# Reordering the routing stage of two MoE phases: early weight splits, weight loads, spare products, first gather

## What is computed

```
t = rmsnorm(h)
grp_prob = softmax(t @ w_grp + b_grp);  p_g, g_idx = top_k(grp_prob, 1)       # 4 groups
q_top, e_local = top_k(softmax(logits of 8 experts in the group), 2)
gates = p_g * q_top / sum(q_top)
for every expert e (32):  y = (silu(x @ w_gate[e]) * (x @ w_up[e])) @ w_down[e]   # 1024 -> 512 -> 1024
h = h + sum over the two chosen experts of gate * y
```

## Time and profile before

| | |
|---|---|
| median of three runs | 2169.26 us (2168.65 to 2170.42) |
| the profiled execution's own time | 2169.74 us |
| its span | 2167.6 us |
| TensorE busy | 1953.3 us, 90% |
| VectorE busy | 1580.9 us, 73% |
| ScalarE busy | 1252.3 us, 58% |
| GpSimd busy | 383.1 us, 18% |
| DMA | 504.67 MB, mean 233 GB/s |
| first instructions of phase 1 and phase 2 | 400.2 us, 1464.4 us |

### The profile page before, as it was taken

The page is one execution under the profiler, slowest core; times in us unless marked ns, Lnnn a source line. Parts: engine busy times, 40 slices in busy tenths (PEclk is TensorE's granted clock), DMA queues, the critical chain, the costliest instruction groups (busy, mean ns, idle before and its releaser), DMA issues. The chain is left out here.

```text
span 2167.6 us, 31724 instructions
## 1 busy us (share of the span) xinstructions
PE 1953.3 (90%) x10658; PEld 1564.4 (72%) x10658; DVE 1580.9 (73%) x1765; ACT 1252.3 (58%) x1530; POOL 383.1 (18%) x677
## 2 busy tenths in 40 slices
PE   4859999849999999999699999995799999999991
PEld 3648777637888888888588766664688888888880
DVE  8996321358999999999752476646588888888885
ACT  6624210427887788888530265534477777777772
POOL 2000000302322222221233000002122222222214
PEclk9979999869999999999799999997799999999995
DMA  3174200529999999999612110006499999999986
GB/s 102 28 70 158 89 1 1 196 95 350 373 386 379 380 381 378 386 389 388 232 53 56 45 45 2 1 1 255 157 357 360 370 380 380 384 383 388 383 310 243
DMA packets 136044, 504.67 MB, mean 233 GB/s; under 512 B 38466, under 2 KB 68498, under 8 KB 84754
## 3 DMA queue, kind: packets, MB, share of 16 engines
q1 hardware_dynamic: 114658, 468.71, 59.1%
q0 software_dynamic: 18432, 33.86, 4.1%
q10 hardware_dynamic: 2880, 1.12, 0.4%
HBM read 488.47 MB, written 47.32 MB: 247 GB/s over the span
## 5 line engine op out<-in xcount | busy, mean ns | idle before, releaser
L1704 DVE TENSOR_TENSOR moe_lo<-moe_raw,moe_hi 128x2048 fp32r<-128x2048 f32 x378 | 860.9, 2292 | 106.8 <-ACT moe_hi L1483 98.1
L1483 ACT CAST moe_hi<-moe_raw 128x2048 fp32r<-128x2048 f32 x374 | 713.4, 1916 | 144.5 <-PE moe_ps_g L1854 67.2
L1852 PE MATMUL moe_ps_g<-moe_hi,moe_x_hi 128*128 128x512 f32 x512 | 210.4, 411 | 7.7 <-DVE moe_x_lo L1709 4.7
L1852 PE MATMUL moe_ps_y<-moe_hi,moe_h_hi 128*128 128x512 f32 x512 | 207.1, 404 | 3.8 <-DVE moe_h_lo L1720 3.8
L1854 PE MATMUL moe_ps_g<-moe_lo,moe_x_hi 128*128 128x512 f32 x512 | 204.1, 399 | 0.0
L1853 PE MATMUL moe_ps_g<-moe_hi,moe_x_lo 128*128 128x512 f32 x512 | 203.9, 398 | 0.0
L1854 PE MATMUL moe_ps_y<-moe_lo,moe_h_hi 128*128 128x512 f32 x512 | 202.1, 395 | 0.0
L1853 PE MATMUL moe_ps_y<-moe_hi,moe_h_lo 128*128 128x512 f32 x512 | 201.8, 394 | 0.0
L1854 PE MATMUL moe_ps_u<-moe_lo,moe_x_hi 128*128 128x512 f32 x512 | 201.2, 393 | 0.0
L1852 PE MATMUL moe_ps_u<-moe_hi,moe_x_hi 128*128 128x512 f32 x512 | 200.8, 392 | 0.0
L1853 PE MATMUL moe_ps_u<-moe_hi,moe_x_lo 128*128 128x512 f32 x512 | 200.8, 392 | 0.0
(11 more groups left out here) (457 smaller groups left out, 3749.9 us busy)
## 6 DMA issues: line engine op xcount, KB each, us to landing
moe_raw<-moe_w_gate SPq DMA_DIRECT2D x128, 1024.0 KB, 7.0
moe_raw<-moe_w_up SPq DMA_DIRECT2D x128, 1024.0 KB, 8.0
moe_raw<-moe_w_down SPq DMA_DIRECT2D x128, 1024.0 KB, 7.5
mix_r<-ssm_w_glu SPq DMA_DIRECT2D x16, 512.0 KB, 5.3
xn_dram<-moe_work SPq DMA_DIRECT2D x16, 512.0 KB, 7.2
prj_yc<-y_dram SPq DMA_DIRECT2D x8, 1024.0 KB, 7.0
moe_raw<-y_dram SPq DMA_DIRECT2D x8, 1024.0 KB, 11.0
mix_r<-x SPq DMA_DIRECT2D x8, 512.0 KB, 5.4
```

The costliest lines, as they stand in the source:

```text
L1483: A.copy(hi[:, slot(number, k), :], raw[:, k, :]).then_inc(hi_done, 1)
L1704: V.tensor_tensor(lo[:, slot, :], raw[:, k, :], hi[:, slot, :].bitcast(F32), ALU.subtract).then_inc(lo_done, 1)
L1852: T.matmul(out, x_h, w_h, start=first, stop=False)
```

## The change

- VectorE waits for the router's bias in `logits(0)`, TensorE for the router's weights in `tile_logits(0)`, not ahead of the loop.
- ScalarE does the squares two tiles ahead.
- `EARLY` is (2, 4, 6), and the six weight loads stand behind the stores of tiles 0, 1, 3, 5, 6, 7 (`LOADS`).
- TensorE makes 8 products of the identity with itself (`spare_products`) ahead of the tile loop and 18 ahead of its register load. Their result is not used.
- The first gather takes its rows from `idx_in[:, 0:1]` directly, without `column`.
- The transposes, the cast and the subtraction of the first expert tile go in two halves; the first piece of the gate product waits for the first half alone.

```
@@ names
+        x0_mm, x0_hi, x0_lo = (sem(x) for x in ("x0_mm", "x0_hi", "x0_lo"))
...
-        EARLY = (5, 6, 7)
+        EARLY = (2, 4, 6)
+        LOADS = (0, 1, 3, 5, 6, 7)
@@ sync
                 sp.dma_start(xn_dram[i * P:i * P + rows(i), :], xn[0:rows(i), i % XB, :]).then_inc(xn_out[i % XB], 16)
-                if i < NB:
-                    load(i, 0)
+                if i in LOADS:
+                    load(LOADS.index(i), 0)
@@ gpsimd
-            def gather(tile, step):
-                column(gi, idx_in, tile, step)
+            def gather(index):
                 G_.indirect_dma_start(xg[:, :], None, xn_dram[:, :],
-                                      bass.IndirectOffsetOnAxis(gi[:, :].bitcast(U32), 0),
+                                      bass.IndirectOffsetOnAxis(index.bitcast(U32), 0),
...
-            gather(0, 1)
+            pool.wait_ge(rows_ready, 1)
+            gather(idx_in[:, 0:1])
             pool.wait_ge(list_ready, 2)
             n_q = pool.value_load(n_more[0:1, 0:1], min_val=0, max_val=XTR) + N_EXP
             for tile in range(1, 3):
                 pool.wait_ge(xt_mm, tile)
-                gather(tile, tile + 1)
+                column(gi, idx_in, tile, tile)
+                gather(gi[:, :])
...
@@ scalar
             squares(0)
+            squares(1)
             for i in range(NT):
-                if i + 1 < NT:
-                    squares(i + 1)
+                if i + 2 < NT:
+                    squares(i + 2)
...
-            x_hi_part(0)
+            act.wait_ge(x0_mm, 1)
+            A.copy(x_hi[:, 0:KC, :].rearrange("p c m -> p (c m)"), ps_xt[:, 0:512]).then_inc(x0_hi, 1)
+            act.wait_ge(xt_mm, 1)
+            A.copy(x_hi[:, KC:, :].rearrange("p c m -> p (c m)"), ps_xt[:, 512:]).then_inc(xt_hi, 1)
@@ vector
-            dve.wait_ge(b_rt_in, 32)
 
             def logits(i):
+                if i == 0:
+                    dve.wait_ge(b_rt_in, 32)
                 dve.wait_ge(lg_mm, i + 1)
...
-            x_lo_part(0)
+            for q, (ready, done) in enumerate(((x0_hi, x0_lo), (xt_hi, xt_lo))):
+                dve.wait_ge(ready, 1)
+                part = slice(KC * q, KC * (q + 1))
+                V.tensor_tensor(x_lo[:, part, :].rearrange("p c m -> p (c m)"), ps_xt[:, 512 * q:512 * (q + 1)],
+                                x_hi[:, part, :].bitcast(F32).rearrange("p c m -> p (c m)"),
+                                ALU.subtract).then_inc(done, 1)
@@ tensor
+            def spare_products(n):
+                for _ in range(n):
+                    T.matmul(ps_u[:, 0:P], ident[:], ident[:], start=True, stop=True)
+
             pe.wait_ge(ident_step, 2)
-            pe.wait_ge(rt_in, 32)
+            spare_products(8)
 
             def tile_logits(i):
+                if i == 0:
+                    pe.wait_ge(rt_in, 32)
...
             last.then_inc(slot_mm, 1)
+            spare_products(18)
             pe.wait_ge(list_ready, 2)
...
-            def transpose_x(e):
+            def transpose_x(e, halves=False):
...
+                    if halves and c == KC - 1:
+                        last.then_inc(x0_mm, 1)
...
-                pe.wait_ge(xt_lo, e + 1)
+                if not halves:
+                    pe.wait_ge(xt_lo, e + 1)
                 for k in range(4):
+                    if halves and k < 2:
+                        pe.wait_ge((x0_lo, xt_lo)[k], 1)
...
-            transpose_x(0)
-            gate_up(0, lambda k: 2 + k, [(2 + k) % 3 for k in range(4)])
+            transpose_x(0, halves=True)
+            gate_up(0, lambda k: 2 + k, [(2 + k) % 3 for k in range(4)], halves=True)
```

More of the change, by code:

```diff
@@ L1429, in _ @@
                 pool.wait_ge(xt_mm, tile)
-                gather(tile, tile + 1)
+                column(gi, idx_in, tile, tile)
+                gather(gi[:, :])
             with pool.Fori(1, n_q - 2) as e:
                 pool.wait_ge(xt_mm, e + 2)
-                gather(e + 2, e * 2 + 2)
+                column(gi, idx_in, e + 2, e * 2 + 1)
+                gather(gi[:, :])
                 pool.wait_ge(y_done, e)
-                scatter(e - 1, e * 2 + 3)
+                scatter(e - 1, e * 2 + 2)
             for last in range(3):
                 pool.wait_ge(y_done, n_q + (last - 2))
-                scatter(n_q + (last - 3), n_q * 2 + (last - 2))
+                scatter(n_q + (last - 3), n_q * 2 + (last - 3))
             if last_layer:
@@ L1854, in products, with gate_up @@
                 return T.matmul(out, x_h, w_l, start=False, stop=final)
-            def gate_up(e, number, slots):
-                pe.wait_ge(xt_lo, e + 1)
+            def gate_up(e, number, slots, halves=False):
+                if not halves:
+                    pe.wait_ge(xt_lo, e + 1)
                 for k in range(4):
+                    if halves and k < 2:
+                        pe.wait_ge((x0_lo, xt_lo)[k], 1)
                     pe.wait_ge(lo_done, number(k) + 1)
```

## The result

The changed kernel takes **2156.93 us** (median of 12 runs; eleven lie between 2153.92 and 2161.79, and one slow run of 2187.62 us is not compared), against 2168.86 us for the kernel before, run beside it on the same chip (12 runs, 2166.46 to 2173.89). The ratio is 0.9946, 95% interval 0.9939 to 0.9953: 11.9 us faster, where 12.2 were forecast. The profiled execution took 2154.48 us, its span is 2152.4 us.

A forecast was written before the change was run, and what follows sets the result against it. It took the expert loop as TensorE-bound and unchanged, with the gains ahead of it: 1.7 + 3.8 + 1.5 + 0.4 + 2.7 + 2.1 = 12.2 us, giving 2157.0 us; range 2152 to 2164.

The forecast's parts named there:

- Entry: Start of each phase's tile loop: transposes of tile 2 (T2) start 2.4 us sooner in phase 1, 3.2 in phase 2.
- Pauses: Tile loop: 1.5 us before transposes of tiles 4, 6, 8; 4.5 us in phase 1, 3.0 in phase 2.
- rival 3: Tile loop: the pauses drop the clock, five at 1.6 us are 8.0 us, 2165.0 us; chance 0.08.
- First load: Cast at tile 2: wait for its weight load between 0 and 3.5 us, taken as 0.
- Transposes of the first expert: Seam: transposes start after 18 spare products (6.0 us) and register load (0.8): 465.15 against 464.48, phase 2 1526.0 against 1524.27.
- Chain in halves: First expert's first transposes to first product: 2.15 us against 4.33; product 1.5 us sooner, phase 2 0.4.
- Clock: First 48 products of the first expert, all at full clock: 2.7 us saved in phase 1, 2.1 in phase 2.
- Rival 1: Seams: 18 spare products at low clock take 8.1 us, outlast the wait; seams lose 4.2 us, 2161.2 us; chance 0.12.
- Rival 2: Tile loop: GpSimd falls behind VectorE, rstd of tiles 5 and 7 late, 4 us, 2161.0 us; chance 0.08.
- Rival 4: Tile loop: clock stays low from tile 4's pause to the end; change slower, net +13, 2182 us; chance 0.03.

The follow-up runs named there:

- the second profile: The changed kernel itself, unedited, timed again beside the kernel before: 2154.85 us, ratio 0.9935.
- the last run: Changed kernel with router-bias wait back ahead of VectorE's loop, router-weights wait ahead of the first transposes, behind the 8 spare products: 2159.75 us, ratio 0.9959.

## Why the prediction was right, point by point

- **Entry.** Forecast 2.4 and 3.2 us for T2; measured 3.22 and 3.10. In phase 1 the 8 products were through at the start of T0 (404.00), and T0 itself ran partly at full clock (1.59 us). The 0.7 us charged for their own time was too much: it is 0 to 0.6 us. The run without them puts their return at 0.4 to 1.4 us per phase, that time included.
- **Pauses.** Forecast 1.5 us each, on the scaling behind a subtraction; measured 1.31, 1.24, 1.23 and 1.52, 1.24. In phase 1 the clock then fell for 1.5 us at L7, which the forecast had left to rival 3; in the second profile it did not. Entry and pauses together: forecast 1.7 and 3.8, measured 1.5 and 4.0.
- **First load.** Forecast no wait; it held in phase 1 with almost nothing to spare, as the last run showed, and within 0.2 us in phase 2. Here luck helped: the forecast's own range for this wait was 0 to 3.5 us. Its remark that SP passes 1 MB at tiles 2 and 4 is a slip, since only the 0.5 MB store is left there.
- **Transposes of the first expert.** Here a step failed: "The register load, 0.48 + 0.16 us on the weight-load queue plus gaps, 0.8 in all, was hidden under the gather and no longer is." It runs while the spare products do, and costs nothing: a term of 1.6 us over both seams that should have been zero. With 5.69 and 6.18 us for the products, where 6.0 was forecast, they start 0.74 us sooner in phase 1 and 0.78 later in phase 2, instead of 0.7 and 1.7 later. The start in phase 1 also needs the sooner gather, which the forecast had put at nothing, hidden under the products: they end at about the time it lands.
- **Chain in halves.** Forecast 2.15 us; measured 2.12 and 2.00. The first product came 3.0 and 1.5 us sooner, against 1.5 and 0.4 forecast: 2.6 us too little. The register load is 1.6 of it, the shorter row of phase 1 another 0.3, and the rest are hand-overs.
- **Clock.** Forecast 2.7 and 2.1 us; measured 2.72 and 1.87. With 6 slow products in both phases, the low end of the 6 to 14 that the Trainium skill gives for one kernel (TensorE: Matmul & The Clock Gate, "What's actually happening"), it would have been 2.2 together, by estimate; the trace measured 4.6. The page does not call 6 the usual count, as the prediction took it.
- **Not forecast.** The tile from the second to the third expert's transposes takes 1.1 us more in phase 1 and 0.25 in phase 2. Its window was 18.64 us at a granted clock of 0.91 before, and 19.77 at 0.83 after. TensorE waits the same in both, 2.96 us for VectorE's `moe_hid` and 1.52 us for a subtraction; only the granted clock behind the first of them differs, 0.88 before and 0.78 after. Both lengths came with a fast and with a slow start of the 48 products ahead of it: 18.64 us in the run with the waits behind the 8 products, whose 48 were fast, and 20.19 without the 18 products, whose 48 were slow. So it is not shown to be the change's doing. It took back 1.4 us, nearly what the register load had given.

So the sum of 12.2 came out at 13.2 by stages and 11.9 by medians. That it came so near is in part luck: the seams returned 2.6 us more than forecast and the second expert's tile took 1.4 back. Rival 1 is half true: in phase 2 the spare products do outlast the gather, by 1.1 to 1.6 us, but they took 5.69 and 6.18 us and not 8.1. Rival 2 did not come up in the changed kernel. Rival 3 came at one pause of five in one profile, 1.5 us and not 8.0. Rival 4 did not come up. What stays open is how much of the 11.9 the late gathers move: one stands in the profile of the kernel before, seven in that of the kernel without the 8 products, and none in either profile of the changed kernel.

Not all parts of the change pay. Against the medians of the changed kernel, squares two ahead are worth 4.5 to 6.6 us (a late load in phase 2 included), the moved waits 2.8 to 4.9, the 8 products 1.2 to 3.2 (1.3 to 1.8 by stages). The 18 products are worth 3.6 to 3.9 us by stages (1.7 by medians) and the halves 5.9 (1.5 to 3.6 by medians); these two overlap, since each needs the other. The direct first gather is worth an estimated 0.7. The placement of splits costs 3.1 us with the squares ahead and 6.0 without. With the scaling ahead of the subtraction that cost is gone, and the kernel takes 2148.83 us. This order with 12 spare products in phase 2 was not run; by an estimate from the stages it should give another 0.8.

## What to carry to other kernels

A step that is spread out to relieve an engine costs its full pause at each place, if it stands in the queue ahead of work for which the next engine waits; put that work first, and then spreading pays. Filling a wait with spare products is free only as far as the wait reaches, so measure the wait in every phase, and look in the trace whether the clock stays up over the wait behind them. Before charging an instruction on a side queue to the path, look whether the main unit has work queued ahead of it.

## What the runs showed of the hardware

- A register load on TensorE's weight-load queue (0.49 us) ran under products that had been issued before it; the transposes followed the last product with no gap.
- Pauses of TensorE of 1.2 to 1.5 us left the clock up in most cases, with a dip behind the third of them in some executions (L7 3.48 us) and not in others (1.94). After 2.12 and 2.13 us it fell each time, in four places at once (transposes 1.75 to 1.97 us, not 1.16) and in phase 2 of the kernel before from the logits on (3.37 us, not 1.94); after 2.36 us it fell within the next 48 products (granted clock 0.86). But after 2.02 us it stayed up twice and after 2.05 it fell, and after 3.30 us it stayed up (transposes 1.16 us). So these runs give no length of pause that decides it.
- A GpSimd instruction of 0.19 us took up to 1.31 us, and one of 0.56 us 1.47 and 2.47 us, beside VectorE's subtractions and scalings. The issue of an indirect DMA took 3.11 and 3.14 us beside subtractions, where 1.04 to 1.06 us is the rule in the same loop. In some executions a gather is late enough for TensorE to wait, 11.8 us in all in one of them. The Trainium skill (SBUF — State Buffer, "Who interferes with whom") has a VectorE instruction with two SBUF inputs contend with a GpSimd instruction that reads SBUF; the trace agrees with that (rstd 2.47 us, not 0.56, beside the subtraction).
